# Turning queries, keys and probabilities of sixteen heads by transposing DMAs instead of TensorE

## What is computed

```
qa, ka, va, qb, kb, vb = split(h @ w_in)          # 8 heads of 128 columns each
qa, ka = rope(qa), rope(ka);  ya = dilated_attention(qa, ka, va)   # "dil" heads
s = einsum(qb_c, kb_c) * (64 ** -0.5)             # c = 0, 1: two halves of 64 columns
p = softmax(s);  a = p[0] - lam * p[1]            # "diff" heads
yb = rmsnorm(a @ vb, subln) * (1 - lam_init)
x = x + concat(ya, yb) @ w_out
```

## Time and profile before

| | before |
|---|---|
| median of 3 runs | 2505.16 us (2504.85 to 2505.3) |
| the profiled execution | 2505.05 us, its span 2503.2 us |
| PE busy | 2496.5 us, 100% of the span |
| DVE, ACT busy | 1444.5 us (58%), 1231.9 us (49%) |
| POOL busy | 422.1 us (17%) |
| DMA queue of the SP | 489.33 MB, 67.5% of 16 engines' time |

### The profile page before, as it was taken

One profiled execution on the slowest core, in us unless ns is written; L12 is line 12 of the kernel. 1 busy time (PEld: TensorE's weight loads), 2 busy tenths in 40 slices (PEclk: granted clock), 3 DMA queues, 4 the chain that ended last, 5 costly groups with the idle time before them and its releaser, 6 DMA issues.

```text
span 2503.2 us, 30775 instructions
## 1 busy us (share of the span) xinstructions
PE 2496.5 (100%) x11260; PEld 2065.3 (83%) x11260; DVE 1444.5 (58%) x1707; ACT 1231.9 (49%) x1698; POOL 422.1 (17%) x379
## 2 busy tenths in 40 slices
PE   9999999999999999999999999999999999999999
PEld 7888888888888888888888888888888888888887
DVE  5555556555555555566445555566567646675665
ACT  6555545444344434455445544544555535553553
POOL 2222213121001101121000111112233103320230
PEclk9999999999999999999999999999999999999999
DMA  8565557776677667676666656667777767776775
GB/s 238 162 173 162 160 176 205 202 210 202 193 201 202 210 193 202 203 224 199 180 183 179 181 180 188 181 187 217 209 210 213 217 194 218 219 210 194 203 224 178
DMA packets 416530, 493.16 MB, mean 197 GB/s; under 512 B 111937, under 2 KB 214949, under 8 KB 416289
## 3 DMA queue, kind: packets, MB, share of 16 engines
q1 hardware_dynamic: 415056, 489.33, 67.5%
q0 software_dynamic: 1088, 2.07, 0.3%
q10 hardware_dynamic: 272, 0.26, 0.0%
HBM read 467.44 MB, written 2.11 MB: 188 GB/s over the span
## 4 chain that ended last, share of the span: by engine, by line
PE 99%; DVE 0%; DMA 0%; SPq 0%; issue 0%; ACT 0%; ACTq 0%
PE ps L518 32%; PE ps L520 32%; PE ps L519 32%; PE ps L613 0%; PE ps L595 0%; PE ps L628 0%; PE ps L601 0%; PE ps L685 0%; PE ps L705 0%; PE ps L768 0%; PE ps L913 0%; DMA raw<-in_w_in 0%; PE ps L638 0%; PE ps L888 0%; PE ps L652 0%
## 5 line engine op out<-in xcount | busy, mean ns | idle before, releaser
L1407 DVE TENSOR_TENSOR w_lo<-raw,w_hi 128x1024 fp32r<-128x1024 f32 x880 | 1110.0, 1263 | 1011.4 <-ACT w_hi L984 1008.5
L984 ACT ACTIVATE w_hi<-raw 128x1024 fp32r<-128x1024 f32 x880 | 930.9, 1059 | 1150.8 <-PE ps L520 1112.1
L518 PE MATMUL ps<-w_hi,xT_hi 128*128 128x512 f32 x2204 | 871.9, 396 | 0.7 <-DVE xT_lo L1426 0.7
L520 PE MATMUL ps<-w_hi,xT_lo 128*128 128x512 f32 x2204 | 859.6, 390 | 0.0
L519 PE MATMUL ps<-w_lo,xT_hi 128*128 128x512 f32 x2204 | 858.3, 389 | 0.0
L518 PE MATMUL ps<-w_hi,yT_hi 128*128 128x512 f32 x1312 | 512.4, 391 | 0.0
L520 PE MATMUL ps<-w_hi,yT_lo 128*128 128x512 f32 x1312 | 510.7, 389 | 0.0
L519 PE MATMUL ps<-w_lo,yT_hi 128*128 128x512 f32 x1312 | 510.6, 389 | 0.0
L520 PEld LDWEIGHTS ps<-w_hi,xT_lo 128*128 128x128 f32 x2204 | 413.7, 188 | 87.3
L518 PEld LDWEIGHTS ps<-w_hi,xT_hi 128*128 128x128 f32 x2204 | 414.0, 188 | 86.3 <-issue 2.7
L519 PEld LDWEIGHTS ps<-w_lo,xT_hi 128*128 128x128 f32 x2204 | 414.2, 188 | 83.3
(11 more groups left out here) (207 smaller groups left out, 884.0 us busy)
## 6 DMA issues: line engine op xcount, KB each, us to landing
raw<-in_w_up SPq DMA_DIRECT2D x264, 512.0 KB, 4.2
raw<-in_w_down SPq DMA_DIRECT2D x176, 512.0 KB, 4.3
raw<-in_w_in SPq DMA_DIRECT2D x160, 512.0 KB, 3.8
raw<-in_w_gate SPq DMA_DIRECT2D x88, 512.0 KB, 4.3
raw<-in_w_out SPq DMA_DIRECT2D x60, 512.0 KB, 4.3
raw<-in_w_in SPq DMA_DIRECT2D x128, 192.0 KB, 2.8
raw<-in_w_in SPq DMA_DIRECT2D x192, 128.0 KB, 2.5
raw<-in_w_proj_m SPq DMA_DIRECT2D x16, 512.0 KB, 3.9
```

Of the source, the lines that this page charges most:

```text
L518: pe.matmul(o, hi[:, q], w_hi[n % NS][:, k, 0:width], start=first, stop=False)
L520: mm = pe.matmul(o, lo[:, q], w_hi[n % NS][:, k, 0:width], start=False, stop=last)
L984: nc.scalar.activation(w_hi[n % NS][:, :, 0:width], raw[n % NS][:, :, 0:width], ACT.Copy).then_inc(hi_ready, 1)
L1407: v.tensor_tensor(w_lo[n % NS][:, :, 0:width], raw[n % NS][:, :, 0:width], f32(w_hi[n % NS][:, :, 0:width]), ALU.subtract).then_inc(lo_rea ...
```

## The change

Queries and keys, and the probabilities, of all sixteen heads are turned the other way: POOL writes the 16-bit halves of `stage` or of `mix`/`prob` into a buffer in a part of `z1` or `z2` that is free at the time (`halve_qk`, `halve_p`), SP sends one transposing DMA for each (128 x 1024 halves, `turn_heads`), and POOL joins the halves into `qkT` or `pT` (`join_qk`, `join_p`). The eight transposes of each head on PE and the three copies on ACT (`qk_out`, `p_out`) are gone. The scale of the diff heads' scores moves from ACT's copy into the exponential, and DVE scales the row maximum by an instruction of its own. Heads begin at unit 14 + 6k, and their steps are: scores after 1, values after 7, output after 11 (diff) or 8 (dil) units. SP asks for head k's queries and keys behind load 17 + 6k and for its probabilities behind load 24 + 6k, and waits there until POOL has halved them.

```diff
-HEAD_STEPS = (0, 1, 4, 5, 8)
-HEAD_FIRST, HEAD_EVERY = 12, 6
+DIFF_STEPS, DIL_STEPS = (1, 7, 11), (1, 7, 8)
+HEAD_FIRST, HEAD_EVERY = 14, 6
+QK_SENT, P_SENT = 3, 10
...
+            def turn_heads(unit):
+
+                for after, bufs, halved_, across_ in ((QK_SENT, qk_bufs, qk_halved, qk_across), (P_SENT, p_bufs, p_halved, p_across)):
+                    k = sent_at(unit, after)
+                    if k is not None:
+                        sp.wait_ge(halved_, k + 1)
+                        split_, flipped_ = bufs[k // HEADS]
+                        sp.dma_start_transpose(flipped_.rearrange("p t e f s -> p (t e f) s"),
+                                               split_.rearrange("p t e n -> p (t e n)")).then_inc(across_, 16)
+
             def load(n, i, step, src, width):
 
                 sp.wait_ge(lo_ready, at(i, n + 1, step))
                 sp.dma_start(raw[n % NS][:, :, 0:width], src).then_inc(raw_landed[n % NS], 16)
+                turn_heads(n + i * step)
...
-                if u == u_qk:
-                    turn_qk(hb, h)
                 if u == u_scores:
-                    pe.wait_ge(hb.qkT, h.upto(2))
+                    pe.wait_ge(hb.qkT, h.upto())
...
-                if u == u_p:
-                    pe.wait_ge(hb.mixed, h.upto(2))
-                    turn_p(hb, mix, FULL_SRC)
...
                         v.tensor_reduce(neg_max[:, :, c], ps[5 + c][:, :].rearrange("p (t s) -> p t s", t=NT), X, ALU.max,
-                                        negate=True).then_inc(hb.row_max, 1)
+                                        negate=True).then_inc(hb.raw_max, 1)
+                        dve.wait_ge(hb.raw_max, h.upto(2, c + 1))
+                        v.tensor_scalar(neg_max[:, :, c], neg_max[:, :, c], B_SCALE, None, ALU.mult).then_inc(hb.row_max, 1)
...
+            def halve_qk(k):
+
+                s, head = (hb, ha)[k // HEADS], k % HEADS
+                pool.wait_ge(s.staged, head + 1)
+                g_.tensor_copy(qk_bufs[k // HEADS][0], stage_halves).then_inc(qk_halved, 1)
+
+            def join_qk(k):
+
+                s, head = (hb, ha)[k // HEADS], k % HEADS
+                pool.wait_ge(qk_across, 16 * (k + 1))
+                pool.wait_ge(hb.scores, 2 * min(k, HEADS))
+                if k > HEADS:
+                    pool.wait_ge(ha.scores, head)
+                g_.tensor_copy(qkT_halves, qk_bufs[k // HEADS][1].rearrange("p t e f s -> p f t s e")).then_inc(s.qkT, 1)
...
             pool.wait_ge(small_landed, 16 * N_SMALL)
             rope_head(hb, Head(0, 0, 0), "in_b", z1, rope_b, 2, 16)
...
+            halve_qk(0)
+            join_qk(0)
+            for k in range(2 * HEADS):
+                if k < HEADS - 1:
+                    rope_head(hb, Head(0, k + 1, 0), "in_b", z1, rope_b, 2, 16)
+                elif k < 2 * HEADS - 1:
+                    if k == HEADS - 1:
+                        pool.wait_ge(late_landed, 16 * N_LATE)
+                    rope_head(ha, Head(0, k + 1 - HEADS, 0), "in_a", z2, rope_a, 1, 32)
+                if k < 2 * HEADS - 1:
+                    halve_qk(k + 1)
+                if 1 <= k <= HEADS:
+                    head_factor(hb, Head(0, k - 1, 0), NT, 2, eps_diff)
+                halve_p(k)
+                if k >= HEADS:
...
+                    stage_v(ha, h, z2, h.num(WH, 2 * P))
+                if k < 2 * HEADS - 1:
+                    join_qk(k + 1)
+                join_p(k)
```

More of the change, by code:

```diff
@@ L163, in heads_at, with sent_at @@
     return [(k // HEADS, k % HEADS, unit - HEAD_FIRST - k * HEAD_EVERY) for k in range(2 * HEADS)
-            if 0 <= unit - HEAD_FIRST - k * HEAD_EVERY <= HEAD_STEPS[-1]]
+            if 0 <= unit - HEAD_FIRST - k * HEAD_EVERY <= DIFF_STEPS[-1]]
+def sent_at(unit, after):
+    k = (unit - HEAD_FIRST - after) // HEAD_EVERY
+    return k if 0 <= k < 2 * HEADS and HEAD_FIRST + k * HEAD_EVERY + after == unit else None
 def evacuated(name, head, groups):
@@ L213, in __init__ @@
         self.coef = one("coef")
+        self.y_coef = one("y_coef")
         self.mixed = one("mixed")
@@ L265, in two_blocks @@
         turned = work[:, 8 * S:12 * S].rearrange("p (f s) -> p f s", s=S)
+        stage_halves, mix_halves, prob_halves = (work[:, c * S:(c + 2) * S].bitcast(U16).rearrange("p (t n e) -> p t e n", t=NT, e=2)
+                                                 for c in (10, 4, 0))
         turned_halves = work[:, 8 * S:12 * S].bitcast(U16).rearrange("p (n e) -> p n e", e=2)
@@ L347, in two_blocks @@
         stored, half_done = sem("stored"), sem("half_done")
[L348 to L351, removed]
+        hb = HeadSems(sem, "diff", ("masked", "v_staged", "qk_T", "p_T"))
+        ha = HeadSems(sem, "dil", ("raw_max", "coef", "sq", "ms", "rstd", "y", "y_T", "qk_T", "p_T", "y_coef"))
+        hm = HeadSems(sem, "mlstm", ("rope", "v_staged", "y_coef"))
+        hf = HeadSems(sem, "fox", ("rope", "row_max", "coef", "y", "y_T", "y_coef"))
         block = ctx.enter_context(nc.Block())
@@ L641, in _ @@
             FULL = {(t, kt): 2 * kt + t for t in range(NT) for kt in range(2)}
-            FULL_SRC = [t * S + kt * P for kt in range(2) for t in range(NT)]
             CAUSAL = {(0, 0): 0, (1, 0): 1, (1, 1): 2}
@@ L788, in residual @@
                               ready=ready, behind=behind, also=also if g else None)
-            residual("out_a", 4, yT, 0, KT, ready=lambda u: pe.wait_ge(ha.y_lo, FREE + UK * (u + 1)))
+            residual("out_a", 4, yT, 0, KT, first=lambda u: heads(112 + u), ready=lambda u: pe.wait_ge(ha.y_lo, FREE + UK * (u + 1)))
             def ffn1():
@@ L1158, in residual @@
                     turn(name, i, 2 * units, behind)
-            residual("out_a", 4, KT, xT_hi, G_FFN, 0)
+            residual("out_a", 4, KT, xT_hi, G_FFN, 0, also=lambda u: heads(112 + u))
             def ffn1():
@@ L1605, in sum_squares @@
                 v.tensor_reduce(ss[:], part_ss[:], X, ALU.add).then_inc(ss_ready, 1)
-            residual("out_a", 4, KT, xT_hi, xT_lo, G_FFN, lambda q: add_fresh("out_a", q, 4, 0))
+            residual("out_a", 4, KT, xT_hi, xT_lo, G_FFN, lambda q: add_fresh("out_a", q, 4, 0), also=lambda u: heads(112 + u))
             def ffn1():
@@ L1932, in _ @@
             pool.sem_inc(slot_used, NS)
[L1934 removed]
+            for s in (by_act, by_dve, tok_lo, act_lo, part_sq, x_kept, *(h.qk_T for h in (hm, hf)), *(h.ms for h in (hb, hm, hf)),
                       *(h.y_lo for h in (hb, ha, hm, hf))):
```

101 lines of the change are left out of this document (51 added, 50 removed).

## The result

The changed kernel takes 2513.56 us (median of 7 runs, 2511.62 to 2517.19), the kernel before 2505.19 (2504.83 to 2505.34). The ratio is 1.0035, interval 1.0025 to 1.0045: 8.4 us slower. The forecast was 2499.0, 6 us faster. The profiled execution has a span of 2510.7 us, 7.5 above that of before. The runs also scatter more: 5.6 us from the fastest to the slowest, where before it was 0.5.

A forecast was written before the change was run, and what follows sets the result against it. TensorE (PE) was taken as the bound, with 99% of the chain. 2505.05 us less 16.3 of PE work plus 10.2 of waits at four heads gave 2499.0, range 2491.5 to 2504.5.

The forecast's parts named there:

- the change part by part: Working that priced work removed, moved and added on PE, ACT, DVE and POOL; PE's gain 16.3 us.
- neither is on the chain: Claim that three copies per head off ACT and two small scalings per diff head on DVE miss the critical chain.
- ahead of the values of heads 0, 4, 8 and 12 alone: Expected trace sign: PE idle only there, released by POOL's joining, longest at head 4.
- the 10.2 of the sum: PE's waits for values at heads 0, 4, 8, 12: 2.1, 4.4, 1.3, 2.05 us, plus 0.1 each for restart.
- The gain of work: On PE: 14.1 us from transposes removed, 2.2 from values standing directly ahead of the next scores; 16.3 together.
- The period of a regular head: On PE, heads without waits follow each other at 18.7 us (diff) and 18.05 us (dil).
- The four heads at an evacuation: Scores of heads 0, 4, 8, 12 meet an evacuation, delaying the next rotation and queue; PE waits 10.2 us in all.
- The clock: Rival: PE, still for over 4 us at head 4, returns at its lower clock; 3 to 5.5 us, chance 0.12.
- The slower case: Rival: transposing DMAs land after more than about 7.5 us, every head waits; 2514 to 2546 us, chance 0.09.
- The regular heads: Twelve of sixteen heads wait for nothing, as joined probabilities have a cover of 3 to 4 us before PE.

The follow-up runs named there:

- the evacuation first: The changed kernel with ACT's evacuation ahead of the head's steps in the same unit; 2495.48 us, ratio 0.9961 to the kernel before.
- the version without waits: The changed kernel with ACT's evacuation ahead of the head's steps and diff heads' outputs scaled two units ahead of their turning; 2489.6 us, ratio 0.9938.
- the filler's: The changed kernel with 17 unused matmuls of ones ahead of head 0's values and 9 ahead of head 3's output; 2515.23 us (with 36 and 18: 2518.09).
- the tables moved: The changed kernel with SP's seven small tables issued behind load 48 and the transposing DMA of head 4's probabilities; 2510.2 us, ratio 1.0023.
- the two placements together: Same kernel as the version without waits: the changed kernel with the edits of evacuation and scaling; 2489.6 us.

## Why the prediction was wrong

**The step that failed** is the one that was not in the working. In "the change part by part" the waits considered were those for what POOL joins. The third move on PE's path, the scaling of the diff heads' outputs from two units ahead of their turning to one, was neither priced nor listed; it stood in the diff. The trace of before gave its price: from ACT's split at 110.53 to the end of DVE's split, where the maxima start at 112.76, there are 2.2 us, to which the coefficient and two scalings add 0.8 (109.58 to 110.38 us in the trace of before): 3.0 against a unit of 2.75. Instead of nothing, the runs show 10.4 us there. 5.6 of them are left with the evacuation first and go with the placement; the rest, at heads 0, 3 and 7, is the coefficient slowed by POOL's copies (2.6) and the norm's factor that stands late in POOL's queue. The prediction named what stands ahead of the moved steps on POOL and SP, and not on DVE. It wrote of the work taken from ACT and added on DVE that "neither is on the chain", and looked for idle time of PE "ahead of the values of heads 0, 4, 8 and 12 alone".

That step is not the whole miss. With the scaling back at its old distance the kernel takes 2508.37 us, still 9.4 above the forecast and outside its range. In that version's trace PE waits 4.2, 4.0, 0 and 1.5 us for the values of heads 0, 4, 8 and 12, 9.7 in all, near the 10.2 of the sum; but 5.0 us more go with the lower clock behind the first two, and 3.1 with the outputs of heads 3 and 7.

**The gain of work**, 16.3 us (14.1 to 17.1): right. 15.5 us are measured, with every wait away. The period of a regular head is 18.8 (diff) and 18.1 us (dil) in the version without waits, 18.7 and 18.05 were said.

**The four heads at an evacuation**: the mechanism was right, the place too, the sizes partly. For head 0, the evacuation ended at +6.2 (6.3 said), the rotation at +10.55 (10.5), halving at +12.65 (11.95), SP's second transposing DMA began at +15.7 (14.65), landed at +19.3 (18.45), the joining ended at +21.55 (19.7); PE came at +17.5 (17.6). Two copies took 2.04 and 2.22 instead of 1.45 and 1.17: a DVE split ran at the same time (67.66 and 76.44 us), and the median was the wrong row for a chain in which splits are always running. For head 4 the chain ended at +24.0 (23.0 said), but PE waited 1.6 and not 4.4 us at the values, as it had already lost 4 at head 3's output. Head 8's wait (1.3) did not come, for the same reason; head 12's was 2.0 (2.05). The sum of waits for values was taken at 10.2 and is 7.8 from 4.15, 1.65 and 2.0. That it comes near is in part luck: head 0's was too small in the sum by 2, head 4's too large by 2.8. A slip of 0.1 us is in the working: 19.09 - 0.88 - 0.1 - 0.16 is 17.95 and not 17.85, so head 12's wait should have stood at 1.95.

**The clock** was a rival with a chance of 0.12, priced at 3 to 5.5 us. It is 4.4 us in the profiled run: 3.0 behind head 0's values, for a wait of 4.15 us that was forecast as 2.1, and 1.4 behind head 3's output. It should have been in the forecast's tail as soon as a single wait of 4.4 us stood in the sum. The Trainium skill, "TensorE: Matmul & The Clock Gate", part 1, says that an idle array falls to the lower clock; the trace agrees (0.50 over 78 to 84 us).

**The slower case** that I named, landings beyond 7.5 us, did not happen: 3.0/3.7/6.2 us in the changed kernel. The regular heads wait for no values, as forecast: the 3.7 us of the longer way are nobody's wait there, and the 0.44 us for each four transposes are saved on PE. The Trainium skill, "VectorE: DVE Perf Modes", section "Rules for kernel authors", advises TensorE for a 128x128 transpose where PSUM will do; here the measurement decides otherwise, the DMA wins 15.5 us as soon as it is asked for early enough.

## What to carry to other kernels

Taking work off the engine that bounds is worth its distance only if everything that this engine meets afterwards is there in time: list all steps whose distance in units changed, the small ones on other engines too, and compare each with the turn in which its engine gets to it. Where an evacuation and a step that waits for another engine stand in one turn, put the evacuation first if something long hangs on it. Waits on one queue don't add up, so remove the head of the queue before filling or shortening the waits at its end. Small instructions count when they stand just ahead of what the bounding engine waits for: here one of 0.15 us took 1.12 beside a copy on another engine. And a queue that waits for one engine holds up all that stands behind it: here SP's wait for POOL made weight loads late.

## What the runs showed of the hardware

A pause of 4.15 us of PE cost another 3.0 us behind it, at a granted clock of 0.50, and one of 2.25 us sometimes cost 1.4 and sometimes nothing: the same kind of pause at head 7's output had none in the changed kernel and one in the filler's. The scatter goes the same way: 5.6 us between runs of the changed kernel, and 0.3 to 1.9 in the five versions whose longest wait at a head is 1.4 us or less. Whether the clock makes that scatter is not shown; the slowed coefficient varies too, at head 0's output 1.12 us in the changed kernel's trace and 0.15 in that of the tables moved, whose program is the same up to there.

DVE's coefficient, an instruction on 128x2 float32 numbers, took 0.15 us alone and 0.97 to 1.13 us where a 16-bit copy of POOL was running when it started: six times of sixteen in the traces of the changed kernel and of the two placements together, and in none of the other ten. It matters which comes first: at head 0's output of the changed kernel POOL's copy started at 94.37 and the coefficient at 94.42 and took 1.12 us; in the kernel with the tables moved the coefficient started at 92.63 and the copy at 92.66, and it took 0.15.

In the profiled run of the evacuation first the granted clock reads 0.95 from end to end, but a unit of twelve matmuls takes the same 2.72 us as elsewhere, and its span of 2494.3 us is 0.4 to 1.1 above those of the four other runs, which read 1.00. A steady reading just below full is not taken as time here.

36 matmuls of 128x128 ones in float32 took 8.2 us, 0.23 each, and show as 72 records; the eight records of a head's values are four matmuls in the same way.
